# Attention scores over the rows that hold data, and two weight splits moved, in a three-block transformer kernel

## The reference

```python
s = (jnp.einsum('bqhd,bkhd->bhqk', qn, k_nope)
     + jnp.einsum('bqhd,bkd->bhqk', qr, k_rope)).astype(jnp.float32) * scale
p = jax.nn.softmax(jnp.where(kpos[None, :] <= qpos[:, None], s, NEG), axis=-1)
```

## Time and profile before

| what | value |
|---|---|
| timed runs | 1940.82, 1939.26, 1940.37 us, median 1940.37 |
| profiled execution | 1935.49 us, of which the span is 1933.7 us |
| TensorE products busy | 1771.7 us (92%) |
| VectorE busy | 1293.5 us (67%) |
| ScalarE busy | 919.1 us (48%) |
| POOL busy | 324.4 us (17%) |
| mean load of the DMA engines | 251 GB/s, 485.02 MB |

### The profile page before, as it was taken

The page is one execution under the profiler, slowest core; times in us unless marked ns, Lnnn a source line. Parts: engine busy times, 40 slices in busy tenths (PEclk is TensorE's granted clock), DMA queues, the critical chain, the costliest instruction groups (busy, mean ns, idle before and its releaser), DMA issues.

```text
span 1933.7 us, 29225 instructions
## 1 busy us (share of the span) xinstructions
PE 1771.7 (92%) x11218; PEld 1413.9 (73%) x11218; DVE 1293.5 (67%) x2402; ACT 919.1 (48%) x1905; POOL 324.4 (17%) x336
## 2 busy tenths in 40 slices
PE   8999999999999999999999988989987787777777
PEld 8999989999999999699998778976432232222222
DVE  5565887556765576976656757886776766766454
ACT  5444555444544453764445436633544344344433
POOL 2000004000000000030000000523433333333331
PEclk9999999999999999999999989999999999999999
DMA  7555425965555545035555423679999999999998
GB/s 289 189 180 188 144 91 149 259 250 183 168 194 195 184 145 189 33 111 198 183 195 165 131 88 110 205 296 379 407 420 422 422 421 422 422 421 420 421 422 321
DMA packets 96139, 485.02 MB, mean 251 GB/s; under 512 B 10577, under 2 KB 10833, under 8 KB 62977
## 3 DMA queue, kind: packets, MB, share of 16 engines
q0 software_dynamic: 38544, 275.25, 37.0%
q1 hardware_dynamic: 57456, 207.90, 32.1%
HBM read 478.65 MB, written 4.46 MB: 250 GB/s over the span
## 4 chain that ended last, share of the span: by engine, by line
PE 58%; DMA 15%; DVE 9%; issue 9%; POOL 5%; ACT 3%; another core or an unknown queue 0%; POOLq 0%; SPq 0%; ACTq 0%; DVEq 0%
PE PS L549 16%; PE PS L550 16%; PE PS L551 16%; DMA raw<-uv,A 4%; PE PS L2212 3%; DMA XF<-uv,A 2%; DMA YL<-uv,A 2%; DMA YH<-uv,A 2%; PE PS L2233 2%; DVE WL L1040 2%; DMA raw<-wst 2%; POOL raw L659 1%; DMA XH<-uv,A 1%; DMA WH<-uv,A 1%; DMA WL<-uv,A 1%
## 5 line engine op out<-in xcount | busy, mean ns | idle before, releaser
L1040 DVE TENSOR_TENSOR WL<-raw,WH 128x1024 fp32r<-128x1024 f32 (+1 forms) x375 | 449.7, 1241 | 88.7 <-ACT WH L676 88.1
L549 PE MATMUL PS<-XH,WH 128*128 128x256 f32 x1616 | 461.1, 285 | 15.2 <-DVE WL L1040 6.5
L550 PE MATMUL PS<-XL,WH 128*128 128x256 f32 x1616 | 456.3, 282 | 0.0
L551 PE MATMUL PS<-XH,WL 128*128 128x256 f32 x1616 | 455.9, 282 | 0.0
L676 ACT ACTIVATE WH<-raw 128x1024 fp32r<-128x1024 f32 (+1 forms) x375 | 370.9, 1041 | 39.0 <-PE PS L551 16.7
L549 PEld LDWEIGHTS PS<-XH,WH 128*128 128x128 f32 x1616 | 306.5, 190 | 19.7 <-DVE A L1431 7.4
L550 PEld LDWEIGHTS PS<-XL,WH 128*128 128x128 f32 x1616 | 306.6, 190 | 0.2
L551 PEld LDWEIGHTS PS<-XH,WL 128*128 128x128 f32 x1616 | 306.4, 190 | 0.0
L983 ACT ACTIVATE A<-A,RTK 128x1 f32<-128x1 f32 x256 | 75.1, 293 | 298.1 <-DVE A L1640 294.9
L726 ACT ACTIVATE A<-A 128x256 f32<-128x256 f32 x88 | 36.8, 418 | 342.2 <-DVE A L1075 342.2
L549 PE MATMUL PS<-GH,WH 128*128 128x256 f32 x704 | 198.2, 282 | 1.1 <-DVE WL L1040 1.1
(11 more groups left out here) (318 smaller groups left out, 2989.3 us busy)
## 6 DMA issues: line engine op xcount, KB each, us to landing
raw<-wst SPq DMA_DIRECT2D x381, 512.0 KB, 4.6
raw<-wst SPq DMA_DIRECT2D x8, 384.0 KB, 3.5
vscr<-A POOLq DMA_DIRECT2D x1, 3072.0 KB, 37.5
A<-vscr POOLq DMA_DIRECT2D x1, 2048.0 KB, 22.4
C<-cst SPq DMA_DIRECT2D x1, 1236.5 KB, 10.5
raw<-uv,A POOLq DMA_INDIRECT x65
hT<-xin SPq DMA_DIRECT2D x2, 512.0 KB, 4.7
A<-vscr POOLq DMA_DIRECT2D x1, 1024.0 KB, 12.5
```

What stands on the lines that cost most here:

```text
L549: pe.matmul(o, wh, xh, start=start, stop=False, skip_group_check=True)
L550: pe.matmul(o, wh, xl, start=False, stop=False, skip_group_check=True)
L551: return pe.matmul(o, wl, xh, start=False, stop=stop, skip_group_check=True)
L1040: dv.tensor_tensor(WL[:, m % SPL, 0:w], raw[:, i % RAW, 0:w], f32(WH[:, m % SPL, 0:w]), ALU.subtract).then_inc(s_lo, 1)
```

## The change

Latent scores: both products of a pair of heads use only the partitions that hold the head's data, 64 for the nope part and 32 for the rope part, and the two heads of a pair alternate inside each query block. For this the columns of the rope weights are laid out in the order of heads 4t, 4t+2, 4t+1, 4t+3, so that an even head's rope queries stand in the first 64 partitions. Sparse scores: 64 partitions each, the heads alternating. All zero fills of key tiles and the waits for them go. In pass 6 the high and low halves of units 2 and 3 of `qa` get calls of their own, ahead of the weighted squares.

```diff
-    rope = [... for h in range(4 * t, 4 * t + 4)]) for t in range(4)]
+    rope = [... for h in (4 * t, 4 * t + 2, 4 * t + 1, 4 * t + 3)]) for t in range(4)]
...
-            po.wait_ge(s_sums, 1)
-            po.memset(KN[0], 0.0)
-            po.memset(KN[1], 0.0)
-            po.memset(KP, 0.0).then_inc(s_pad, 1)
...
-            po.memset(KSW[0], 0.0)
-            po.memset(KSW[1], 0.0).then_inc(s_pad, 1)
...
                     high_x(p, kc)
+                    if p == 6 and kc == 7:
+                        hi("qa", 2, 0)
...
                 if p == 6:
+                    hi("qa", 3, 0)
                     for kc in range(8):
                         ac.activation(XF[:, kc, :], hT[:, kc, :], ACT.Square,
...
-                ac.wait_ge(s_pad, 1)
...
                 low_x(p, 7)
+                if p == 6:
+                    lo("qa", 2, 0)
                 pairs(p)
+                if p == 6:
+                    lo("qa", 3, 0)
...
-                    dv.wait_ge(s_pad, 1)
...
-            dv.wait_ge(s_pad, 2)
...
-                for e in range(2):
-                    h = 2 * j + e
-                    for blk in range(2):
-                        o = PS[:, b0 + e, 128 * blk:128 + 256 * blk]
-                        kk = slice(0, 128 + 128 * blk)
-                        qs = slice(128 * blk, 128 * blk + 128)
-                        pe.matmul(o, QN[:, j, qs], KN[e][:, j, kk], start=True, stop=False, skip_group_check=True)
-                        ins = pe.matmul(o, QR[:, h // 4, qs], KP[:, h % 4, kk], start=False, stop=True, skip_group_check=True)
+
+                for blk in range(2):
+                    kk = slice(0, 128 + 128 * blk)
+                    qs = slice(128 * blk, 128 * blk + 128)
+                    for e in range(2):
+                        r = slice(64 * e, 64 * e + 64)
+                        pe.matmul(PS[:, b0 + e, 128 * blk:128 + 256 * blk], QN[r, j, qs], KN[e][r, j, kk], start=True, stop=False,
+                                  skip_group_check=True)
+                    for e in range(2):
+                        i = 2 * e + j % 2
+                        r = slice(32 * i, 32 * i + 32)
+                        ins = pe.matmul(PS[:, b0 + e, 128 * blk:128 + 256 * blk], QR[r, j // 2, qs], KP[r, i, kk], start=False,
+                                        stop=True, skip_group_check=True)
...
-                for e in range(2):
-                    for blk in range(2):
-                        ins = pe.matmul(PS[:, b0 + e, 128 * blk:128 + 256 * blk], Q[:, j, 128 * blk:128 * blk + 128],
-                                        KSW[e][:, 2 * m + j // 4, 0:128 + 128 * blk], start=True, stop=True, skip_group_check=True)
+                for blk in range(2):
+                    for e in range(2):
+                        r = slice(64 * e, 64 * e + 64)
+                        ins = pe.matmul(PS[:, b0 + e, 128 * blk:128 + 256 * blk], Q[r, j, 128 * blk:128 * blk + 128],
+                                        KSW[e][r, 2 * m + j // 4, 0:128 + 128 * blk], start=True, stop=True, skip_group_check=True)
```

More of the change, by code:

```diff
@@ L73, in plan @@
     nope = [np.concatenate([96 * h + ar(64) for h in (2 * t, 2 * t + 1)]) for t in range(8)]
-    rope = [np.concatenate([96 * h + 64 + ar(32) for h in range(4 * t, 4 * t + 4)]) for t in range(4)]
-    rops = [np.concatenate([96 * h + 64 + (ar(32) + 16) % 32 for h in range(4 * t, 4 * t + 4)]) for t in range(4)]
+    rope = [np.concatenate([96 * h + 64 + ar(32) for h in (4 * t, 4 * t + 2, 4 * t + 1, 4 * t + 3)]) for t in range(4)]
+    rops = [np.concatenate([96 * h + 64 + (ar(32) + 16) % 32 for h in (4 * t, 4 * t + 2, 4 * t + 1, 4 * t + 3)]) for t in range(4)]
     for t in range(4):
@@ L416, in program @@
                                                                  "hidden_low", "down"))
-        s_pad = sem("zeroed")
         s_c5, s_c5q, s_c5s, s_rn, s_cn, s_yh, s_yl = (sem(n) for n in ("c_out", "c_squares", "c_sums", "c_root", "c_normed",
```

## The result

The changed kernel took 1929.07 us (median of 5 runs, 1923.62 to 1930.26) against 1939.94 (5 runs, 1937.20 to 1940.82) on the same chip: ratio 0.994, interval 0.9926 to 0.9954. Of 1939.94 us that is 8.9 to 14.4 us less, 11.6 in the middle, where the prediction summed up 8.75 and forecast 1931.6. The profiled execution of after is its median run: 1929.07 us with a span of 1927.3, against 1935.5 and 1933.7 for before, which was faster than any of the five timed runs of before.

What follows compares the result with a forecast made beforehand. TensorE, busy for 92% of the span, was taken to bound the kernel. Latent scores 3.9, sparse scores 0.45 and second mixer 4.4 summed to 8.75 us, so 1940.4 became 1931.6 us, range 1928 to 1936.8.

Steps and rivals of the forecast that it cites:

- the prediction's three places: Latent scores, sparse scores and second mixer, forecast to gain 3.9, 0.45 and 4.4 us.
- Latent scores: Latent attention: a pair of heads takes 2.11 us against 2.62, the step 3.72; 3.9 us gained.
- The disputed price, 64 to 32 rows: Latent scores: going from 64 to 32 rows counts as a change of shape, 0.20 us each.
- Rival 1: Latent scores: 64 to 32 rows is free, VectorE limits the gain to 5.4 us; 1930.1 us, chance 0.10.
- Rival 2: Latent scores: quarters do not overlap or changes cost over 0.2; stage loses 1.3 us, 1936.8 us, chance 0.12.
- Sparse scores: Sparse attention: nothing in the loop, which VectorE paces; first set starts 0.45 us sooner, bounds 0 and 0.78.
- Rival 4: Sparse loop: TensorE does less, its clock drops to 1.2 GHz, +1.7 us a step; 1954 us, chance 0.05.
- Second mixer: Second mixer's opening: TensorE's 3.65 us idle gap goes, clock regained, root 4.4 us sooner; bounds 2.9 and 5.2.
- the copy hangs on the root alone: Second mixer: VectorE's chain from root to copy takes 9.03 us; 0.8 us of 5.2 becomes TensorE waiting.
- the 1.2 of idle time: Second mixer: a sign, some 1.2 us of TensorE idle before the value products.
- Rival 3: Between second mixer and gathers: shifted clock drops, up to 3 us either way around 1931.6; within the forecast's 0.73.
- The fills: POOL's zero fills near the kernel's start: removing them gains zero, since no queue is held by them.

Runs made afterwards that it cites:

- e5: The changed kernel with the latent halves of both query blocks first, then the quarters of both: 1924.27 us, ratio 0.9931.
- e6: The changed kernel with the rope products on 64 rows too and three of five zero fills and their waits back: 1926.37 us, ratio 0.9942.
- e4: The changed kernel once more, on the same chip as its three parts run alone: 1919.70 us, ratio 0.9944.
- e7: e5 with VectorE's copy of the reciprocal roots ahead of one low half instead of behind it: 1925.92 us, ratio 0.9938.
- e8: The changed kernel with latent products one head after the other instead of alternating: 1972.72 us, ratio 1.0178.
- e1: The kernel before with only the new rope column order and new latent scores: 1925.87 us, ratio 0.9981.
- e3: The kernel before with only the mixer's four new calls for early halves of units 2 and 3: 1925.68 us, ratio 0.9973.
- e2: The kernel before with only the sparse scores on 64 rows: 1930.16 us, ratio 0.9996.
- e10: The changed kernel once more, on one chip with e11: 1919.55 us, ratio 0.9948.
- e9: e6 with latent products one head after the other instead of alternating: 1918.31 us (one run).
- e11: e5 once more, on one chip with e10: 1917.62 us, ratio 0.9941.

## Why the prediction was right

It was, in its direction, its mechanisms and nearly in its size: 1929.07 us lies within its range and 2.5 us from its number. Part of that nearness is luck: the prediction's three places are each right within 0.4 us, but what lies outside them moved by more (2.8 us in the traced pair).

**Latent scores: 3.98 us for 3.9.** The pair costs 2.11 us and the step 3.72, both as worked out. The disputed price, 64 to 32 rows, is 0.20 like the other changes: counting the one ahead of the pair, after has four changes and 2.11, e5 two and 1.71, e6 that one alone and 1.51. Rival 1 is false as it stands, but its arithmetic was right: where changes are taken out, VectorE limits, and the gain is the 5.4 that it named (5.5 and 5.7 measured). Rival 2 is false too: the quarters of two heads share their time (a head alone 2.08, both together 2.11). The Trainium skill says in TensorEngine Tiling (Array Packing), Key Properties, that changing the mode drains the engine; the 0.20 per change of after, e5 and e6 agree with it, and put a price on it.

**Sparse scores: 0.45 us for 0.45,** at the start alone. A set takes the 0.85 us that the prediction gave it (798.48 to 799.33 in e4). The loop keeps VectorE's pace in every run where the clock stayed up.

**Rival 4** may have been right in its mechanism and was wrong in its size. With halved scores the granted clock fell to 0.50 inside the loop in after, e7 and e8, and not in the seven other profiles with halved scores; before, e1 and e3, with full scores, never had it. It stayed down for 6.8 us each time and not for thirteen steps, and VectorE lost 0.6 us in each of the three. Three of ten against none of three is too few to call the fall the edit's doing; it would take more profiles of e2 to tell.

**Second mixer: 4.79 us for 4.4,** and 4.8 in every profile with this edit (5.2 in e7, where the copy moves up too). The gap is gone, the clock there at 1.00, the root right behind the table load. Two terms were mis-sized by little. The root came 4.57 sooner, not 4.4: it is the wait of 4.57 that the earlier trace rows show in front of the root, which the prediction rebuilt from rounded pieces. And I wrote that the copy hangs on the root alone, 9.03 us behind it; in before it stood 9.03 behind because TensorE's last products came late, and VectorE's own chain is 8.81 (1055.57 to 1064.38). So TensorE waits 0.65 us for the copy, 0.4 more than the 0.25 of before and not 0.8 more, and less than the 1.2 of idle time that the prediction named as a sign.

What the prediction did not see is that the fall of the clock comes back. All ten profiles with the mixer's edit have 3.4 us at 0.50 in the sliding-window attention (1090.10 to 1093.50 in after), and before, e1 and e2, which have it at 1050 to 1058, have none there. In after it costs TensorE 1.4 us (6.62 early, then 5.21 early), and they are won back at once in its waits for VectorE (6.73 early at 1098.46), so it cost no time here.

**Rival 3** holds as the spread that it was put as. From the copy to shortly ahead of the first gather, with no edit in between, VectorE wins 2.3 us in e3 and 1.4 in after and loses 0.7 in e4 and 1.3 in e2, with the falls of the clock at other places in each.

**The fills: 0 for 0** (e6 has three of the five back, with their waits).

**Open.** The three measured terms give 3.98 + 0.45 + 4.79 = 9.2 us, and the ratio says 11.6 (8.9 to 14.4), e4 10.8 and e10 10.0. All three intervals hold 9.2. Two traces from one chip say where such a surplus can come from: e4 ends 10.6 us ahead of e2, which has the sparse edit too, and beside 3.98 and 4.9 in the latent stage and the mixer there are 0.5 us from the first instruction on, 0.7 in the stretches near 360 and 699 us, and 0.6 between the mixer and the gathers, none of them at an edited place. Whether the edits bring these about isn't settled.

Where the chips differ stands in the traces as well. Before takes 1940 us beside after and 1938 beside e5 to e8, but 1931 beside e1 to e4 and 1930 beside e9 to e11. In these last two groups every run, whatever its edit, wins 4.4 us against the trace of before over the first gathers (1262 to 1285 us) and some 2.4 more by 1400.

## What to carry to other kernels

Products that fill only half or a quarter of the rows are worth giving to separate rows and issuing alternately, but count the changes of shape first: each cost 0.20 us here, as much as a product of 128 columns, and grouping by shape gives half of them back for nothing. Before splitting a product, look at which engine ends each step: 0.45 us came from sixteen halved sets where VectorE sets the pace. And in a queue that feeds the next stage, put the one half that the idle engine waits for ahead of work that is only summed later, which gave 4.8 us; then follow it to the next wait, here the root behind the table load and the copy behind the root, which kept 0.4 of TensorE's 5.2 us.

## What the hardware showed beyond that

TensorE's clock fell in a stretch where its records leave no gap: 36.60 of 36.60 us busy at a granted 0.50 in e8, behind 4.4 us at 1.00, with one head on 64 or 32 rows at a time and a change of shape after every product. The same products with two heads abreast had 1.00 in after and, in another order, in e5. A full busy column is thus no promise of the full clock.

Here products on other rows started ahead of older ones only while the shape stayed: in e9 (one shape) head 1 starts 0.55 us behind head 0, in e8 (two shapes) it waits for all of head 0, 2.08 us.
